# Final norm by token halves, roots spread from stride-zero weights, and the convolution's middle tap on ScalarE, in a kernel of two transformer-like blocks

## The reference

```python
def rms_norm_2(x, g):
    x32 = x.astype(jnp.float32)
    y = x32 * lax.rsqrt(jnp.mean(x32 * x32, axis=-1, keepdims=True) + RMS_EPS)
    return (y * g.astype(jnp.float32)).astype(x.dtype)
...
        h = rms_norm_2(x, g_ffn[l])
        up = depthwise_conv(h @ w_up[l], conv_f_w[l], conv_f_b[l], FFN_CONV // 2)
        act = jax.nn.gelu(up[..., :D_FF_2], approximate=True) * up[..., D_FF_2:]
        x = x + act @ w_down[l]
    return rms_norm_2(x, g_final)
```

## Time and profile before

| | |
|---|---|
| median of 3 runs | 1875.42 us (1874.94 to 1876.23) |
| profiled execution, its own time | 1876.3 us |
| its span, first to last instruction | 1874.5 us |
| PE busy | 1851.7 us, 99% of the span |
| DVE busy | 1239.2 us, 66% |
| ACT busy | 528.6 us, 28% |
| POOL busy | 15.4 us, 1% |
| mean granted clock of TensorE | 0.996 of full speed |
| data moved | 194.64 MB, 104 GB/s over the span |

### The profile page before, as it was taken

How to read it: one execution, slowest core, us unless ns; L and a number is a source line. 1 busy time by engine, 2 the same in 40 slices (tenths; PEclk the granted TensorE clock), 3 DMA queues, 4 the chain that set the end, 5 groups by cost and what they waited for, 6 DMA issues and landing times.

```text
span 1874.5 us, 21498 instructions
## 1 busy us (share of the span) xinstructions
PE 1851.7 (99%) x8588; PEld 1479.1 (79%) x8588; DVE 1239.2 (66%) x1662; ACT 528.6 (28%) x489; POOL 15.4 (1%) x57
## 2 busy tenths in 40 slices
PE   8999999999999999999999999999999999999997
PEld 6888888878888778888888888876778888788875
DVE  6764667667745577443345789979975698726874
ACT  5333222122332232221121111158842122212210
POOL 0000000000000000000000000000000000000000
PEclk9999999999999999999999999999999999999998
DMA  5224341473211332222322234232224232232221
GB/s 204 90 81 154 113 157 64 146 254 111 68 68 46 123 124 90 95 96 84 107 90 76 84 103 144 88 113 90 70 77 157 90 104 93 69 116 90 81 73 70
DMA packets 48132, 194.64 MB, mean 104 GB/s; under 512 B 6720, under 2 KB 15296, under 8 KB 33344
## 3 DMA queue, kind: packets, MB, share of 16 engines
q1 hardware_dynamic: 48064, 193.70, 30.1%
HBM read 180.84 MB, written 12.85 MB: 103 GB/s over the span
## 4 chain that ended last, share of the span: by engine, by line
PE 78%; issue 20%; DVE 2%; DMA 0%; ACT 0%; POOLq 0%; POOL 0%; DVEq 0%; SPq 0%; ACTq 0%
PE bank L951 24%; PE bank L953 24%; PE bank L952 24%; PE xb L1227 2%; PE xb L1173 0%; PE xb L1163 0%; DVE wlo L1302 0%; PE bank L1068 0%; PE bank L1069 0%; PE bank L1070 0%; PE xb L1181 0%; PE xb L990 0%; PE xb L983 0%; DVE x L1346 0%; PE xb L1129 0%
## 5 line engine op out<-in xcount | busy, mean ns | idle before, releaser
L951 PE MATMUL bank<-uhi,whi 128*128 128x512 f32 x1552 | 622.2, 401 | 6.8 <-DVE wlo L2153 6.6
L953 PE MATMUL bank<-uhi,wlo 128*128 128x512 f32 x1552 | 616.1, 397 | 0.0
L952 PE MATMUL bank<-ulo,whi 128*128 128x512 f32 x1552 | 616.0, 397 | 0.0
L656 ACT ACTIVATE whi<-raw 128x2048 fp32r<-128x2048 f32 (+3 forms) x177 | 299.9, 1694 | 1086.5 <-PE bank L953 1057.8
L1302 DVE TENSOR_TENSOR wlo<-raw,whi 128x2048 fp32r<-128x2048 f32 (+3 forms) x177 | 356.6, 2015 | 80.9 <-ACT whi L656 78.4
L951 PEld LDWEIGHTS bank<-uhi,whi 128*128 128x128 f32 x1552 | 293.0, 189 | 79.8 <-issue 9.3
L953 PEld LDWEIGHTS bank<-uhi,wlo 128*128 128x128 f32 x1552 | 292.8, 189 | 71.4
L952 PEld LDWEIGHTS bank<-ulo,whi 128*128 128x128 f32 x1552 | 293.2, 189 | 70.8 <-issue 1.4
L951 PE MATMUL bank<-hhi,whi 128*128 128x512 f32 x528 | 210.4, 398 | 2.3 <-DVE hlo L1355 1.2
L952 PE MATMUL bank<-hlo,whi 128*128 128x512 f32 x528 | 210.0, 398 | 0.0
L953 PE MATMUL bank<-hhi,wlo 128*128 128x512 f32 x528 | 209.8, 397 | 0.0
(11 more groups left out here) (387 smaller groups left out, 1800.4 us busy)
## 6 DMA issues: line engine op xcount, KB each, us to landing
raw<-in_up SPq DMA_DIRECT2D x65, 1024.0 KB, 4.8
raw<-in_win SPq DMA_DIRECT2D x16, 1024.0 KB, 4.9
raw<-in_wout SPq DMA_DIRECT2D x8, 1024.0 KB, 4.8
raw<-in_down1a SPq DMA_DIRECT2D x8, 768.0 KB, 4.4
tab<-tab_kept SPq DMA_DIRECT2D x4, 1536.0 KB, 8.7
raw<-in_down2a SPq DMA_DIRECT2D x8, 768.0 KB, 4.3
raw<-in_down3a SPq DMA_DIRECT2D x8, 768.0 KB, 4.4
raw<-in_down1b SPq DMA_DIRECT2D x8, 640.0 KB, 3.9
```

What stands on the lines that cost most here:

```text
L656: act.activation(whi[s][:, 0:width], raw[s][:, 0:width], ACT.Copy).then_inc(w_hi, 1)
L951: pe.matmul(dst, wh, hi, start=first, stop=False)
L952: pe.matmul(dst, wh, lo, start=False, stop=False)
L953: return pe.matmul(dst, wl, hi, start=False, stop=last)
```

## The change

Three edits in one. First, the diagonals go: TensorE takes the roots' column itself as weights, read with stride zero as 128 equal columns, against the identity. It waits for GpSimd's `rs_ready`. In the second mixer both spreads stand at k=1 of unit 1. Second, in the third FFN ScalarE computes middle tap plus bias (`middle_taps`), and VectorE adds the other two. For the last up unit of a half, ScalarE does the taps ahead of the high copy of the second down unit. Third, the last two down units (`last_pair`) are computed for tokens 0 to 255 and then for 256 to 511, so that the first half's norm runs beside the second half's products; the last tile's square is summed by itself. The output leaves as eight DMAs of two tiles by half the tokens.

```diff
-            for k in range(KD):
-                sp.wait_ge(out_ready, k + 1)
-                sp.dma_start(out[k * P:(k + 1) * P, :], x[:, k, :]).then_inc(stored, 16)
+            for t in range(2):
+                tok = slice(t * S // 2, (t + 1) * S // 2)
+                for k in range(0, KD, 2):
+                    sp.wait_ge(out_ready, KD * t + k + 2)
+                    sp.dma_start(out[k * P:(k + 2) * P, tok].rearrange("(m p) s -> p m s", p=P), x[:, k:k + 2, tok])\
+                        .then_inc(stored, 16)
...
-            def inverse_root(width=4):
+            def inverse_root(width=4, at=0):
                 pool.wait_ge(rt_ready, norms.step())
-                pool.tensor_tensor(out=nstat[:, 0:width], in0=nstat[:, 0:width], in1=nstat[:, 8:8 + width],
-                                   op=ALU.pow).then_inc(rs_ready, 1)
+                pool.tensor_tensor(out=nstat[:, at:at + width], in0=nstat[:, at:at + width],
+                                   in1=nstat[:, 8:8 + width], op=ALU.pow).then_inc(rs_ready, 1)
...
-            inverse_root()
+            inverse_root(2, 0)
+            inverse_root(2, 2)
...
+            def middle_taps(nb, turns, m):
+                s = nb % 2
+                for half, dst in ((0, cva), (1, cvb)):
+                    if half:
+                        act.wait_ge(evac[s], nb // 2 + turns)
+                    else:
+                        act.wait_ge(conv_half, n_halves.step())
+                    tap = vec[:, bass.ds(VECS["conv_f_w_2"] + 44 + 22 * half + m, 1)]
+                    bias = vec[:, bass.ds(VECS["conv_f_b_2"] + 22 * half + m, 1)]
+                    act.activation(dst[:, s, :], conv_src[:, half, :], ACT.Identity, scale=tap, bias=bias)\
+                        .then_inc(tapped, 1)
...
+                                if taps:
+                                    middle_taps(nb + j, it, 2 * it + (j - 2 + sum(HALVES[:h])))
                                 gate_tile(nb + j, func)
...
-                            high(nb + j, it, tiles * P)
+                            late = taps and j and isinstance(it, int) and it == 0
+                            if not late:
+                                high(nb + j, it, tiles * P)
                             if isinstance(it, int) and it == 0:
+                                if taps:
+                                    middle_taps(nb - tiles + j, tiles // 2, tiles - 2 + j + sum(HALVES[:h]))
+                                if late:
+                                    high(nb + j, it, tiles * P)
                                 gate_tile(nb - 2 + j, func)
...
+            def root_columns(to, at, width=4):
+                for c in range(width):
+                    last = pe.matmul(XB[to][:, c * P:(c + 1) * P],
+                                     nstat[:, at + c:at + c + 1].broadcast_to([P, P]), ident[:, :],
                                      start=True, stop=True)
-                last.then_inc(spread, 1)
+                return last
+            def spread_roots():
+                pe.wait_ge(rs_ready, n_root.step())
+                root_columns(1, 0).then_inc(spread, 1)
+            def spread_two():
+                pe.wait_ge(rs_ready, n_root.step())
+                pe.wait_ge(roots_made, 1)
+                root_columns(1, 4).then_inc(spread, 1)
+                root_columns(2, 0).then_inc(spread, 1)
...
+            def last_pair(nb, tiles):
+                for t in range(2):
+                    tok = slice(t * S // 2, (t + 1) * S // 2)
+                    for j in range(2):
+                        s = (nb + j) % 2
+                        if t == 0:
+                            pe.wait_ge(w_lo, nb + j + 1)
+                            pe.wait_ge(evac[s], (nb + j) // 2)
+                        for k in range(tiles):
+                            if t == j == 1 and k == 1:
+                                half_spread(0)
+                            if j and k == 6:
+                                half_sums(t, acc, acc_ready, nacc)
+                            if t and j == 0 and k == 4:
+                                half_sums(0, sq, last_sq, n_sq)
+                            last = product(DB[s][t][:, 0:S // 2], (whi[s], wlo[s]), slice(k * P, (k + 1) * P),
+                                           hhi[:, k, tok], hlo[:, k, tok], k == 0, k == tiles - 1)
+                        last.then_inc(tail_out, 1)
+                half_sums(1, sq, last_sq, n_sq)
+                half_spread(1)
...
+            def half_sums(t, src, ready, tally):
+                pe.wait_ge(ready, tally.step())
+                for c in range(2 * t, 2 * t + 2):
+                    at = c if src is acc else 4 + c
+                    last = pe.matmul(XB[2 * t][:, at:at + 1], src[:, c * P:(c + 1) * P], ones[:, 0:1],
+                                     start=True, stop=True)
+                last.then_inc(sums_out, 1)
+            def half_spread(t):
+                pe.wait_ge(rs_ready, n_root.step())
+                for c in range(2 * t, 2 * t + 2):
+                    last = pe.matmul(XB[2 * t + 1][:, c * P:(c + 1) * P],
+                                     nstat[:, c:c + 1].broadcast_to([P, P]), ident[:, :], start=True, stop=True)
+                last.then_inc(spread, 1)
...
-                between[1] = {1: [spread_roots], 5: [lambda: spread_roots(2)]}
+                between[1] = {1: [spread_two]}
...
-            ffn(nb)
-            sum_squares()
-            spread_roots()
+            ffn(nb, ends=True)
...
                 means(XB[0][:, 0:4], D)
-                diagonals(0)
                 dve.wait_ge(spread, n_spread.step())
-            def diagonals(at):
-                for c in range(4):
-                    last = dve.tensor_scalar(diag[:, c, :], ident[:, :], nstat[:, at + c:at + c + 1], None, ALU.mult)
-                last.then_inc(diag_ready, 1)
             def prepare(gain, m):
...
-                dve.tensor_tensor(out=conv_src[:, 0, :], in0=DB[s][0][:, :], in1=inv[:, :], op=ALU.mult)
+                dve.tensor_tensor(out=conv_src[:, 0, :], in0=DB[s][0][:, :], in1=inv[:, :], op=ALU.mult)\
+                   .then_inc(conv_half, 1)
                 dve.tensor_tensor(out=conv_src[:, 1, :], in0=DB[s][1][:, :], in1=inv[:, :], op=ALU.mult)\
                    .then_inc(evac[s], 1)
...
-                    bias = vec[:, bass.ds(VECS["conv_f_b_2"] + 22 * half + m, 1)]
-                    then(dve.tensor_scalar(dst[:, s, :], src, tap[1], bias, ALU.mult, ALU.add))
+                    dve.wait_ge(tapped, taps_made.step())
...
+                    if ends and h == 1:
+                        last_pair(nb + KD - 2)
+                    else:
+                        down_turn(KD // 2 - 1, following)
...
+            def last_pair(nb):
+                tt, ts, stt = dve.tensor_tensor, dve.tensor_scalar, dve.scalar_tensor_tensor
+                def add_in(t, j):
+                    m, tok = KD - 2 + j, slice(t * S // 2, (t + 1) * S // 2)
+                    dve.wait_ge(tail_out, 2 * t + j + 1)
+                    then(tt(out=x[:, m, tok], in0=DB[(nb + j) % 2][t][:, 0:S // 2], in1=x[:, m, tok], op=ALU.add))
+                    square = tt(out=sq[:, tok], in0=x[:, m, tok], in1=x[:, m, tok], op=ALU.mult)
+                    if j:
+                        square.then_inc(last_sq, 1)
+                    else:
+                        then(square)
+                        tt(out=acc[:, tok], in0=acc[:, tok], in1=sq[:, tok], op=ALU.add).then_inc(acc_ready, 1)
+                def part_means(t):
+                    dve.wait_ge(sums_out, n_norm.step())
+                    ts(nstat[:, 4 + 2 * t:6 + 2 * t], XB[2 * t][:, 2 * t:2 * t + 2], 1.0 / D, EPS, ALU.mult, ALU.add)
+                def half_root(t):
+                    dve.wait_ge(sums_out, n_norm.step())
+                    stt(out=nstat[:, 2 * t:2 * t + 2], in0=XB[2 * t][:, 4 + 2 * t:6 + 2 * t], scalar=1.0 / D,
+                        in1=nstat[:, 4 + 2 * t:6 + 2 * t], op0=ALU.mult, op1=ALU.add).then_inc(rt_ready, 1)
+                def scaled(t, ms):
+                    tok = slice(t * S // 2, (t + 1) * S // 2)
+                    for m in ms:
+                        stt(out=x[:, m, tok], in0=x[:, m, tok], scalar=col("g_final_2", m), in1=XB[2 * t + 1][:, tok],
+                            op0=ALU.mult, op1=ALU.mult).then_inc(out_ready, 1)
+                add_in(0, 0)
+                part_means(0)
+                add_in(0, 1)
+                half_root(0)
+                add_in(1, 0)
+                dve.wait_ge(spread, n_spread.step())
+                scaled(0, range(6))
+                part_means(1)
+                add_in(1, 1)
+                scaled(0, range(6, KD))
+                half_root(1)
+                dve.wait_ge(spread, n_spread.step())
+                scaled(1, range(KD))
...
-                    dve.wait_ge(rs_ready, n_rs.step())
```

(37 more changed lines are left out.)

22 lines of the change are left out of this document (11 added, 11 removed).

## The result

The changed kernel takes **1870.41 us** (median of 8 runs, 1868.76 to 1871.45) where the kernel before took 1876.01 on the same chip (median of 8, 1874.94 to 1878.76). The ratio is 0.9968, with a 95% interval of 0.9957 to 0.9979: faster by 3.9 to 8.1 us. The forecast was 1868.2 in a range of 1867.2 to 1871.7, so the time lies in the range, 2.2 us above the forecast: 5.6 us were gained by the medians where 7.2 were expected. (The forecast was reckoned from a median of 1875.42 for the kernel before, 0.6 lower than here.) The profiled execution took 1870.59 us, of which 1868.4 are its span, 6.1 less than the span before.

What follows compares the result with a forecast made beforehand. TensorE, busy 99% of the span, was taken as the bound. Gains of 0.88 + 0.92 + 1.64 + 3.75 = 7.2 us took 1876.3 to 1869.1, and 0.9 to the median gave 1868.2 us; range 1867.2 to 1871.7.

Steps and rivals of the forecast that it cites:

- The passages: Third FFN, two changes from up to down units: taps on ScalarE make splits earlier, gaining 0.88 and 0.92 us.
- The clock at the second passage: Third FFN, second change from up to down units: with less standing TensorE's clock stays up, gaining 1.64 us.
- The end: Last pair of down units and final norm by token halves: last scaling 3.84 us earlier, gain 3.75 us.
- The 0.35 for products of half the width: Last pair of down units: 120 products of 256 columns take 14.40 us for 14.05, +0.35.
- the four inserts: Among the last pair's products: three pairs of sums and one pair of spreads, 4 x 0.525 = 2.10 us.
- The chain after the last product: Final norm's second half: sums, power, spread and eight scalings end 6.74 us after the last product.
- The last transfer: Output's end: same bytes in rows half as long, 0.1 us more; bounds 0 and a halved rate.
- Clock not kept: Rival, 0.15: standing of 0.24 and 0.44 us in the second passage still lets the clock fall; 1869.9 us.
- Output bound: Rival, 0.08: at the end, rows of 1 KB run at half of 379 GB/s; 1870.5 us.
- Taps no use: Rival, 0.12: ScalarE's taps come late or need table loads of 1.283 us; only the end gains, 1871.7 us.
- Slow loads: Rival, 0.05: stride-zero weight loads in the norms' spreads are slow; at three times today's 0.13 us, 1888 us.

## Why the prediction was right, and where it was off

**The passages.** Right in mechanism and nearly in size: 0.84 + 0.84 where 0.88 + 0.92 was forecast. The taps take 802 ns (0.81 expected), and the table loads at the gate are still six. VectorE gains 0.84 in both passages and not 0.92. Its second scaling ends 0.60 behind the first where 0.68 was reckoned, so it stands longer for the tap, and it goes on only 0.10 after the tap's end: 0.26 saved on the first half in place of 0.35. On the second half it is 0.59 (0.57). The Trainium skill, "ScalarE: Activation LUTs", section "Table sets: the hidden batching unit", has identity in every set, and the trace agrees: six loads with the taps as without.

**The clock at the second passage: the term that was too large.** The prediction took 1.64 us for a loss that the kernel before always has, because its one profile had it, and took the standing ahead of it for the cause. The stands are there in every profile of a kernel with VectorE's taps, the fall in two of five. Even where it came it cost 1.54 us, since 0.11 of the 1.64 is the longer first distance behind a stand, which the changed kernel has as well. On the average of the kernel before it is worth about 0.4 x 1.54 = 0.6 us. With shorter stands it never came in eight profiles, so the change does seem to remove it; only the price was too high by about 1.0 us. Two in five against none in eight is also what chance gives now and then, so that even this is likely rather than shown.

**The clock in the second mixer.** Not in the sum, and as far as the runs go rightly so: the fall comes in both kernels, in one of two profiles of each. In the two profiles compared first, before had none and after had one, so a reading of this pair alone would charge 1.5 us to the change. Only more profiles of the same kernels showed that it isn't.

**The end.** Mechanism right, undersized: 4.28 us in place of 3.75. The pair of units took 16.49 us from its first product to the end of the last, against 14.22: 2.27 more for 2.55 predicted. The 0.35 for products of half the width was not there: they are 0.117 apart, not the 0.120 of the row I had taken, so 119 distances and the last 0.28 make 14.2. Three of the four inserts cost 0.45 each instead of 0.525 (from the product before to the second product after 0.68 or 0.69 where two distances are 0.23), and the first 0.85, since it waited 0.30 for VectorE and not 0.1; together 2.2, as in the sum. The chain after the last product was right to 0.2: its power took 0.70 (0.69), the last spread 1.06 (0.6; 0.71 in other profiles), the eight scalings 3.22 (3.24). The last transfer was 0.35 us shorter where I had added 0.1. The rows of 1 KB run at 324 to 343 GB/s where rows of 2 KB made 379, but fewer bytes seem to be left when the last scaling ends; which of the two sizes, of rows or of DMAs, does it was not tried.

**Outside the span.** 2.15 us in place of 1.78 for the kernel before, 0.37 lost that no step of the prediction has. It goes with the taps on ScalarE and is open.

**The sum again**, with what was measured: 0.84 + 0.84 + 0.6 (the fall, on average) + 4.3 (the end) - 0.4 (outside the span) = 6.2 us, against 5.6 by the medians and 3.9 to 8.1 by the ratio. So the forecast came within 1.6 us in part by luck: the 0.5 that the end gave beyond its term covered the 0.4 outside the span, which had no term.

**The rivals.** Clock not kept: not so (0 of 8), though its time, 1869.9, came nearest, for another reason. Output bound: the queues are full at the end, but nothing is late by it. Taps no use: refuted by the passages. Slow loads: refuted by 1.05 us for eight.

**The best version** by the medians is the changed kernel with the sums apart: 1868.5 us on two chips, 0.4% under the kernel before. That it is faster than the changed kernel itself is likely, by the missing wait and fall in its profiles, and not shown by the times.

## What to carry to other kernels

A loss of clock that one profile shows is a draw, not a property of the kernel: before it goes into a sum, or into an explanation, see whether a second execution with the same waits has it. Spread what leaves TensorE thin (one-column matmuls, short waits) over the stream; that this keeps the clock is likely here, and not shown. Take care that what is made later isn't needed sooner; shortening the chain behind it first is what made that free here. At the end of a kernel, where nothing overlaps, halving the granularity of everything (products, sums, power, scalings, transfers) was worth twice all the rest.

## What was not expected of the hardware

TensorE's clock fell from 2.4 to 1.2 GHz for some 3.4 us in the middle of a stream that is otherwise dense, behind 0.3 us of waiting and 16 one-column records (1.95 us); it did so in 4 of 8 profiles with the same wait and the same records there. What decides between the two outcomes no run shows. The clock's sum was 1.70 or 1.71 lower each time, here and behind the stands of the second passage, which at half speed makes the 3.4 us. The price in time was 1.5 us, because products of 512 columns are 0.43 apart at the low level and 0.234 at the high one, less than twice.

GpSimd's power on a tile with 128 partitions takes 0.70 us for two columns, 1.01 for four and 1.64 for eight: cutting it in halves pays when only the second half is waited for.

The time outside the span differs between kernels (1.68 to 1.86 us with all taps on VectorE, 2.05 to 2.20 with the middle ones on ScalarE), though the taps stand far from either end. No view of the trace shows why.
